# Loops written out, the last down and output projections by token chunk, five barriers out and x loaded at once, in a one-core decoder layer

## What is computed

```python
def layer(l, x, attend, x0_re, x0_im):
    x = x + 0.5 * swiglu(rmsnorm(x, g_ffn1[l]), w1_gate[l], w1_up[l], w1_down[l])
    h = rmsnorm(x, g_mix[l])
    q, k, v, qi, ki, wi, u, gates = jnp.split(h @ w_in[l], PROJ_SPLITS, axis=-1)
    o_a = attend(l, q, k, v, qi, ki, wi).reshape(b, t, D_ATTN)   # top-k sparse attention
    y_s, xr, xi = s5_scan(u, ...)                                 # state space branch
    y_s = jax.nn.gelu(y_s)
    o_b = y_s * jax.nn.sigmoid(y_s @ w_glu[l] + b_glu[l])
    g_a, g_b = jnp.split(jax.nn.sigmoid(gates), 2, axis=-1)
    merged = g_a * (o_a @ w_pa[l]) + g_b * (o_b @ w_pb[l])
    x = x + merged @ w_out[l]
    x = x + 0.5 * swiglu(rmsnorm(x, g_ffn2[l]), w2_gate[l], w2_up[l], w2_down[l])
    return x, (k, v, ki, xr, xi)
```

## Time and profile before

| | |
|---|---|
| Median of 3 runs | 3167.9 us (3166.7 to 3173.63) |
| Profiled execution, span from first to last instruction | 3174.7 us |
| PE busy | 2761.3 us, 87% of the span |
| DVE, ACT, POOL busy | 42%, 22%, 26% |
| Chain that ended last, by engine | PE 54%, DVE 11%, issue 3%, ACT 3% |
| Executed instructions | 40,963 |

### The profile page before, as it was taken

The page is one execution under the profiler, slowest core; times in us unless marked ns, Lnnn a source line. Parts: engine busy times, 40 slices in busy tenths (PEclk is TensorE's granted clock), DMA queues, the critical chain, the costliest instruction groups (busy, mean ns, idle before and its releaser), DMA issues.

```text
span 3174.7 us, 40963 instructions
## 1 busy us (share of the span) xinstructions
PE 2761.3 (87%) x16047; PEld 2514.3 (79%) x16047; DVE 1319.7 (42%) x2743; ACT 688.8 (22%) x1195; POOL 817.9 (26%) x521
## 2 busy tenths in 40 slices
PE   5999999999679999956689845688879999999996
PEld 4999999999658999944444544577869999999995
DVE  2223222222338999958731355133351222222224
ACT  4211111110133333313332410221041111111103
POOL 2522233232231112224300060022143232322210
PEclk8999999999889999976689555598989999999998
DMA  3211111110211322232222011142011111111101
GB/s 93 67 40 41 41 48 60 40 53 13 97 27 54 93 80 93 87 146 80 80 106 80 29 11 16 45 174 80 14 49 58 41 56 52 41 53 40 41 14 54
DMA packets 182798, 189.56 MB, mean 60 GB/s; under 512 B 18524, under 2 KB 164176, under 8 KB 179784
## 3 DMA queue, kind: packets, MB, share of 16 engines
q1 hardware_dynamic: 162632, 133.19, 14.0%
q0 software_dynamic: 2944, 35.65, 3.0%
q10 hardware_dynamic: 17072, 18.51, 1.6%
HBM read 160.10 MB, written 25.78 MB: 59 GB/s over the span
## 4 chain that ended last, share of the span: by engine, by line
PE 54%; DVE 11%; issue 3%; ACT 3%; DMA 1%; POOL 1%; SPq 0%; ACTq 0%; DVEq 0%; POOLq 0%
PE ps L232 15%; PE ps L574 12%; PE ps L248 8%; PE ps L1822 3%; PE ps L1808 3%; PE ps L1205 2%; PE ps L802 2%; DVE k_index_T_high L1122 1%; PE ps L824 1%; DVE new_small L1120 1%; PE ps L1522 1%; DVE probs L848 1%; PE ps L1562 1%; PE ps L1492 1%; PE ps L1520 1%
## 5 line engine op out<-in xcount | busy, mean ns | idle before, releaser
L232 PE MATMUL ps<-normed_split,f_weights_split 128*128 128x344 f32 x6336 | 1016.0, 323 | 26.0 <-issue 13.9
L232 PEld LDWEIGHTS ps<-normed_split,f_weights_split 128*128 128x128 f32 x6336 | 1011.0, 190 | 28.9 <-issue 15.3
L248 PE MATMUL ps<-f_hidden_split,f_down_split 128*128 128x344 f32 x3168 | 505.1, 321 | 11.9 <-issue 11.9
L248 PEld LDWEIGHTS ps<-f_hidden_split,f_down_split 128*128 128x128 f32 x3168 | 502.1, 189 | 12.4 <-issue 12.4
L279 DVE TENSOR_TENSOR f_hidden<-f_silu,ps 128x344 f32<-128x344 f32 x132 | 67.7, 513 | 877.3 <-PE ps L232 868.9
L574 PE MATMUL ps<-normed_split,in_weights_split 128*128 128x344 f32 (+1 forms) x2520 | 408.1, 323 | 14.8 <-POOL normed_split L110 13.6
L574 PEld LDWEIGHTS ps<-normed_split,in_weights_split 128*128 128x128 f32 (+1 forms) x2520 | 399.9, 188 | 19.3 <-POOL normed_split L110 14.3
L289 DVE SCALAR_TENSOR_TENSOR x_T<-ps,x_T 128x344 f32<-128x344 f32 x528 | 272.9, 517 | 232.5 <-PE ps L248 232.4
L196 POOL TENSOR_TENSOR f_hidden_split<-f_hidden,f_hidden_split 128x344 fp32r<-128x344 f32 x132 | 122.7, 930 | 595.4 <-DVE f_hidden_split L282 595.4
L188 POOL TENSOR_TENSOR f_weights_split<-f_weights_raw,f_weights_split 128x1024 fp32r<-128x1024 f32 x88 | 210.3, 2410 | 81.9 <-ACT f_weights_split L150 81.9
L202 POOL TENSOR_TENSOR f_down_split<-f_down_raw,f_down_split 128x1024 fp32r<-128x1024 f32 x44 | 104.2, 2388 | 436.2 <-ACT f_down_split L166 436.2
(11 more groups left out here) (303 smaller groups left out, 2624.7 us busy)
## 6 DMA issues: line engine op xcount, KB each, us to landing
f_weights_raw<-in_w_gate SPq DMA_DIRECT2D x44, 512.0 KB, 3.9
f_weights_raw<-in_w_up SPq DMA_DIRECT2D x44, 512.0 KB, 4.2
f_down_raw<-in_w_down SPq DMA_DIRECT2D x44, 512.0 KB, 3.5
in_weights_raw<-in_w_in SPq DMA_DIRECT2D x34, 512.0 KB, 3.8
gates_T<-projected ACTq DMA_DIRECT2D x16, 516.0 KB, 2.6
gates<-gates_T SPq DMA_DIRECT2D x16, 516.0 KB, 4.5
x_meanwhile<-x_T SPq DMA_DIRECT2D x1, 4128.0 KB, 15.1
x_T<-x_meanwhile SPq DMA_DIRECT2D x1, 4128.0 KB, 17.7
```

The source lines that it names most:

```text
L232: mm = nc.tensor.matmul(m.ps[:, NCH * half + c, :CH], m.wh[:, 2 * e + half, a, k * P:(k + 1) * P], m.xn[:, k, b, cols(c)], start=(k == 0 a ...
L248: mm = nc.tensor.matmul(m.ps[:, 6 + n % 2, :CH], m.dh[:, e, a, o * P:(o + 1) * P], m.hh[:, 2 * par + e, b, cols(c)], start=(e == 0 and t = ...
```

## The change

1. **Loops written out.** All `Fori` loops of the feed-forward blocks and of the input projection become straight code on all engines. The order of the work in them is the same.
2. **Last down projection by chunk.** `down(10)` of both blocks goes chunk by chunk (c outside, o inside) through five PSUM banks. From its second chunk on, each group of six matmuls is followed by one of the next norm's sums (`norm_sum`). Its weights are split into free room of the gate and up weights (`wh`), once `gate_up(20)` has ended. DVE adds the third chunk's groups between the multiplications of the next norm's first chunk. "d3" of the output projection likewise.
3. **Norm order on ACT.** Squares run 11 ahead, then one square follows each high part.
4. **Output stage.** The output weights have two buffers, and their splits stand earlier in the streams of SP, ACT and POOL (`SPLITS`); PE keeps `ORDER`.
5. **Barriers** 1, 2, 3, 7 and 8 go; semaphores on x (`ffn_x_ready`, `out_x_ready`) and on the last uses of memory take their place.
6. **Start.** x has a buffer for each block, so all loads are issued at once, the page table behind them on SP; the gains move to ACT's queue. The sums of chunk 0 stand between the turns of blocks 5 and 6. The 8 gathers of POOL move from barrier 3 to the start, ahead of the first weight splits.
7. **End.** The final norm starts in the last down projection; ACT does all its squares and roots ahead of the row copies, and there are four row buffers.

The diff, cut to its core:

```diff
+LAST = NPAIR - 1
+LAST_BANKS = (0, 1, 2, 6, 7)
+SUM_BANK = 3
...
+def norm_act(nc, act, m, s, ready, before=lambda n: None):
+
+    def square(n):
+        c, k = divmod(n, KD)
+        ready(act, c, k)
+        if n >= 3:
+            act.wait_ge(s.sum, s.was.sum + n - 2)
+        nc.scalar.activation(m.sg[:, n % 3, :], m.x[:, k, cols(c)], ACT.Square).then_inc(s.sq, 1)
+
+    for n in range(KD + 3):
+        square(n)
     for c in range(NCH):
         act.wait_ge(s.var, s.was.var + c + 1)
         nc.scalar.activation(m.rstd[:, 1, :], m.rstd[:, 0, :], ACT.Sqrt).then_inc(s.std, 1)
         for k in range(KD):
             n = c * KD + k
             act.wait_ge(s.xn, s.was.xn + n + 1)
             nc.scalar.activation(m.xn[:, k, 0, cols(c)], m.hf[:, n % 3, :], ACT.Copy).then_inc(s.hi, 1)
-
+            if n + KD + 3 < NCH * KD:
+                square(n + KD + 3)
...
+def norm_sum(nc, pe, m, s, n, bank=SUM_BANK):
+    c, k = divmod(n, KD)
+    pe.wait_ge(s.sq, s.was.sq + n + 1)
+    nc.tensor.matmul(m.ps[:, bank + c, :CH], m.ones[:], m.sg[:, n % 3, :],
+                     start=(k == 0), stop=(k == KD - 1)).then_inc(s.sum, 1)
...
+def norm_dve(nc, dve, m, s, gain, bank=SUM_BANK, between=lambda k: None):
     for c in range(NCH):
+        norm_rstd(nc, dve, m, s, c, bank)
         for k in range(KD):
+            if c == 0:
+                between(k)
...
-    def down(p, par, used=True):
+    def down_one(p, o, c, bank, w):
+        for e in range(2):
+            for t, (a, b) in enumerate(PASSES):
+                mm = nc.tensor.matmul(m.ps[:, bank, :CH], w[:, e, a, o * P:(o + 1) * P],
+                                      m.hh[:, (2 * p + e) % 4, b, cols(c)],
+                                      start=(e == 0 and t == 0), stop=(e == 1 and t == 2))
+        mm.then_inc(s.down, 1)
+
+    def down(p):
...
-    with pe.Fori(0, (NPAIR - 3) // 2) as i:
-        for q in range(2):
-            f = 4 * i + 2 * q + 6
-            gate_up(f, 0)
-            gate_up(f + 1, 1)
-            down(2 * i + q + 2, q)
-    down(NPAIR - 1, 0)
+                down_one(p, o, c, 6 + n % 2, m.dh)
+
+    def down_last():
+        pe.wait_ge(s.hlo, s.was.hlo + NCH * NF)
+        pe.wait_ge(s.dlo, s.was.dlo + NF)
+        for n in range(NCH * KD):
+            c, o = divmod(n, KD)
+            if n >= 3:
+                pe.wait_ge(s.acc, s.was.acc + NCH * KD * LAST + n - 4)
+            down_one(LAST, o, c, LAST_BANKS[n % 5], m.wh)
+            if c:
+                next_sum(n - KD)
+        for k in range(KD):
+            next_sum((NCH - 1) * KD + k)
+
+    for f in range(NF):
+        gate_up(f)
+        if f % 2 and f > 1:
+            down(f // 2 - 1)
+    down_last()
 
...
+    for f in range(NF):
+        hidden(f)
+        if f % 2 and f > 1:
+            accumulate(f // 2 - 1)
+    for n in range(2 * KD):
+        ffn_accumulate_last(nc, dve, m, s, n)
...
+SPLITS = (0, 1, 2, "d0", 3, 4, "d1", 5, 6, "d2", 7, "d3")
...
+    odd = sb("out_weights_split_odd", [P, 2, 2, D], F32R)
-    m.dh = sb("out_weights_split", [P, 2, 2, D], F32R)
+    m.dh = (sb("out_weights_split", [P, 2, 2, D], F32R), odd)
...
-                if p:
-                    act.wait_ge(s.down, NCH * KD * p)
-                nc.scalar.activation(m.dh[:, e, 0, :], m.dr[:, e, :], ACT.Copy).then_inc(s.dhi, 1)
+                if p >= 2:
+                    act.wait_ge(s.down, NCH * KD * (p - 1))
+                nc.scalar.activation(m.dh[p % 2][:, e, 0, :], m.dr[:, e, :], ACT.Copy).then_inc(s.dhi, 1)
...
             for n in range(NCH * KD):
-                o, c = divmod(n, NCH)
-                if p or n >= 2:
+                o, c = divmod(n, NCH) if p < 3 else (n % KD, n // KD)
+                if p < 3 and (p or n >= 2):
                     pe.wait_ge(s.acc, NCH * KD * p + n - 1)
+                if p == 3 and n >= 3:
+                    pe.wait_ge(s.acc, NCH * KD * p + n - 4)
+                bank = 6 + n % 2 if p < 3 else LAST_BANKS[n % 5]
+                if p == 3 and c:
+                    next_sum(n - KD)
+    for k in range(KD):
+        next_sum((NCH - 1) * KD + k)
...
+            if p == 3:
+                for n in range(2 * KD):
+                    out_accumulate_last(nc, dve, m, s, n)
+                continue
...
 def in_sp(nc, sp, m, s, i):
-    for n, g in enumerate(i.gains):
-        sp.dma_start(m.grow[KD * n:KD * (n + 1), :], g.rearrange("(k p) -> k p", p=P)).then_inc(s.gain_in, 16)
     for b in range(NB + 1):
         rows = P if b < NB else TS
-        if b >= 2:
-            sp.wait_ge(s.turned, 2 * (b - 1))
         src = i.x_prompt[b * P:(b + 1) * P, :] if b < NB else i.x_sample
-        sp.dma_start(m.xin[:rows, b % 2, :], src).then_inc((s.x_in0, s.x_in1)[b % 2], 16)
+    rows = PAGE // PER_ROW
+    for j in range(N_PAGES):
+        sp.dma_start(m.pages[rows * j:rows * (j + 1), :],
...
+def in_pe(nc, pe, m, s, first_sum):
+    for b in range(6):
+        in_turn(nc, pe, m, s, b)
+    for k in range(KD):
+        first_sum(k)
+    for b in range(6, NB + 1):
+        in_turn(nc, pe, m, s, b)
+    for n in range(KD, NCH * KD):
+        first_sum(n)
+    pe.wait_ge(s.kept, 2 * NB + 2)
...
+def in_act(nc, act, m, s, i):
+    for n, g in enumerate(i.gains):
+        act.dma_start(m.grow[KD * n:KD * (n + 1), :], g.rearrange("(k p) -> k p", p=P)).then_inc(s.gain_in, 16)
...
+    for n in range(KD + 3):
+        square(n)
+    root(0)
+    for n in range(KD + 3, 2 * KD + 3):
+        square(n)
+    root(1)
+    for n in range(2 * KD + 3, NCH * KD):
+        square(n)
+    root(2)
...
+        if b >= 4:
+            act.wait_ge(s_io.y_out[b % 4], s_io.y_from[b % 4] + 16 * (b // 4))
...
+            in_act(nc, act, m_in, s_io, i)
+
+            def blocks_of_x(n):
+                if n in (0, 3, KD):
+                    for b in range(3):
+                        in_keep(nc, act, m_in, s_io, 3 * (0, 3, KD).index(n) + b)
+                if n == KD:
+                    for half in range(2):
+                        ffn_act_split(nc, act, m_f1, s_f1, 0, half)
+            norm_act(nc, act, m_f1, s_f1, x_in_ready, blocks_of_x)
...
+            pool.wait_ge(s_io.steps, 3)
+            for b in range(TS):
+                smp_load(pool, m_mix, b, m_mix.kidx[:, b], i.cache_kidx, s_io.ki_in)
+            for half in range(2):
+                ffn_pool_split(nc, pool, m_f1, s_f1, 0, half)
+            norm_pool(nc, pool, m_f1, s_f1)
             ffn_pool(nc, pool, m_f1, s_f1)
...
+            pool.wait_ge(s_f1.down, NCH * KD * NPAIR)
             nc.gpsimd.memset(m_mix.bias01[:], 0.0).then_inc(s_io.leave, 1)
...
+            in_pe(nc, pe, m_in, s_io, lambda n: norm_sum(nc, pe, m_f1, s_f1, n, 4))
+            ffn_pe(nc, pe, m_f1, s_f1, lambda n: norm_sum(nc, pe, m_mix, s_nm, n))
+            proj_pe(nc, pe, m_mix, s_mix, s_nm)
             barrier(pe, 1)
```

728 lines of the change are left out of this document (321 added, 407 removed).

## The result

The changed kernel takes 3034.7 us (median of 4 runs, 3033.7 to 3036.8), the kernel before in the same comparison 3168.1; the ratio is 0.9564 (95% interval 0.9542 to 0.9585). That is 133 us won where 151 were forecast: the time lies in the range of the prediction, 18 us above the forecast of 3016.9. The profiled execution has a span of 3032.1 us and a time of 3033.9, so 1.8 us of a time lie outside the span; PE is busy for 2741.1 us (90%), and 38,694 instructions were executed.

The account below looks back on a forecast made before the run. PE was taken as the bound, time to be had only at its stops: jumps, output-projection parts and four norms. Six terms, 23.3 + 36.2 + 34.3 + 18.6 + 19.8 + 18.8 = 151.0, took 3167.9 to 3016.9 us; range 2998 to 3046.

Parts of the forecast that it names:

- A: Feed-forward loops: straight code removes PE's stops at jumps back and the slow matmuls after them; 23.3 us, bounds 18 and 25.
- the first part: Opening on what bounds the kernel: stage differences against the profiled execution, span 3174.7 us, are carried over to the median.
- B: Output stage: earlier weight splits with two buffers remove PE's waits ahead of "d0" to "d3" and slow starts; 36.2 us.
- C: Norm between FFN1's last down projection and the input projection: sums between matmuls, no split wait; 34.3 us, bounds 29 and 38.
- D: Norm from "d3" of the output projection to FFN2's first gate tile: shorter chain; 18.6 us, bounds 14 and 22.
- E: Program's end, from FFN2's last down projection through the final norm and stores: shorter; 19.8 us, bounds 14 and 23.
- T0: Last projection before a norm: moment when chunks 0 and 1 with 8 sums end, put at its start S + 19.9.
- F: Program's start up to gate tile 0's end: x loaded at once, first norm earlier; 18.8 us, bounds 8 and 22.
- rival (1): Start: POOL's gathers hold the first norm up, POOL reaching it at 52 instead of 41.5; 3027 us, chance 0.13.
- Rival (2): Interleaved groups and sums: PE's clock falls, about 11 us more in each of C, D and E; 3050 us, chance 0.10.
- (4): Loops: the jumps weren't the cause, stops recur at the same places and A is nothing; 3040 us, chance 0.05.
- rival (3): Written-out code: not fetched in time, each added packet stops PE like a jump; about 3490 us, chance 0.03.

Follow-up runs that it names:

- PE's loop alone: The changed kernel with the hardware loop put back on PE alone in both feed-forward blocks, other engines keeping straight code; 3051.4 us.
- the second one: The kernel before, unchanged, profiled once more; 3166.0 us, span of the profiled execution 3165.9.
- one buffer: The changed kernel with one buffer for the split output weights, split at the old place in the streams of SP, ACT and POOL; 3070.0 us.
- the sums behind: The changed kernel with all 24 next-norm sums behind the last group of the last down and output projections, all additions to x ahead of the norm; 3052.0 us.
- the gathers later: The changed kernel with POOL's 8 gathers moved from the start into FFN1, one behind each of hidden tiles 1 to 8; 3026.7 us.
- the run with 12 spare matmuls: The changed kernel with 12 spare matmuls ahead of the last index projection, gaps ahead of the scores left empty; 3024.4 us, the profiled execution 3006.9.

## Why the prediction was right, and where it was off

**A, right in mechanism, of uncertain size.** The stops are PE's jumps (24.8 us with PE's loop alone), and straight code has none. The size is no constant: 23.3 in the execution read, 16.7 in the second one (10.1 of stops and 4 slow starts), 24.8 with PE's loop alone. The step that failed is the last one of the first part, "I carry the difference over to the median": the terms were read in an execution 8.4 us above the median, and a large part of that was the term itself.

**B, right.** 34.6 in the trace, 35.3 by undoing it, 36.2 forecast. The difference is mostly that "d0" and "d1" hold PE for 23.4 us each (0.50 of it the wait for DVE) and "d2" for 23.0, where 22.8 was taken.

**C, D and E, right step by step.** Ahead of the input projection T0, POOL's three starts, the twelfth sum and the last sum all came within 0.3 us of the forecast. In E the last products end at T0 + 27.3 (27.7) and the program at T0 + 35.2 (35.4). D is 2.4 over its term, since gate tile 0 ran at 22.8 us, at the full clock, where 9.4 was taken for its first chunk, the time at the lower one, and the last sum came at T0 + 24.0. The interleaving is worth 17 us of the three, measured; how order by chunk, the free split and the missing barriers share the other 59 was not tested.

**F, right in its size by luck.** The forecast had POOL and the norm's chain ready together, at 41 and 41.5. POOL was (41.25), by two errors that met: its gathers began at 23.6 and not at 26, and the eighth stopped for 3.24, for which nothing was put. The chain was not: the first high part was done at 33.9, 7 us sooner, since DVE's inversion ended at 32.7 and not at 40.5. So the gathers did hold the first norm up, which is rival (1), not by the stop of the eighth (3.24 us, not 10.6) but by standing there at all; the price is 8.0 us by the run that moved them. What the loads at once and the other edits of the start are worth by themselves was not tested.

**Rival (2) had the right thing at the wrong place.** The clock did not fall among the interleaved groups, as the stretch from the start of the last projection to the end of its groups shows, here in C (D and E have 1.00 there too):

```profile
784.00:817.00 33.00, 31.80 (x177) 28.54 (x176) 19.39 (x34) 12.42 (x25) 6.23 (x6) 1.00 0.00 1
```

It fell 60 us later, in the scores, and cost 10.9. The prediction looked for a lower clock only where the change moves instructions; the scores were not touched, and so no term and no rival spoke of them.

**Rivals (3) and (4) fell.** Straight code shows no idle time without a releaser; the queue that answers to the earlier trace rows has 126 packets, for 119 before, where rival (3) had estimated some 96 more:

```profile
q8 instruction: 126, 2.06, 0.3%
```

In sum, of the 17.6 us between forecast (151.0) and measurement (133.4), 11.4 are losses outside the terms (10.9 of them the scores' clock) and 9.2 the two executions read; the terms gave 3.1 back (0.1 is rounding).

## What to carry to other kernels

Write an engine's long loop out where that engine is the bound, and put the reductions of the next stage between the last matmuls of this one; cost such a chain instruction by instruction from the profile: ahead of the input projection it came out within a microsecond. Check each input of it as well, since the start's chain was 7 us off by the same way of reckoning. Don't carry a difference of spans over to a median before a second execution has been seen: where stops at jumps come and go, one profile can be 8 us off. And list each stretch of narrow or broken PE work behind the change, even an untouched one: its clock may come out at the other level.

## What the runs showed of the hardware

PE's clock in unchanged work is a matter of its own. The 40 score matmuls ran at 1.00 in eight of the traces named above (27 to 28 us from the first to the last) and at 0.50 for most of the stretch in four (38 to 40 us: the changed kernel and the runs with one buffer, with the sums behind and with the gathers later), with the same score instructions. In three of the eight spare matmuls fill the gaps; in the other five the gaps are those of the four. Nor did the level ahead decide: the dense projection in front began at the lower clock in the kernel before (24.52 us) and in the run with the gathers later (24.48, where the changed kernel has 22.96), and the scores behind it ran at 1.00 in the first and at 0.50 in the second. Once down, the clock stayed at 0.50 although PE was busy: here in the tail of attention, behind the 32 one-column matmuls, first in the changed kernel and then in the run with 12 spare matmuls, where it rose again and the stage became 17 us shorter (716.3 instead of 733.6):

```profile
1700.00:1720.00 20.00, 20.00 (x59) 11.30 (x59) 5.83 (x26) 9.81 (x25) 0.00 (x0) 0.50 0.00 0
1720.00:1740.00 20.00, 20.00 (x62) 11.37 (x61) 6.08 (x30) 11.10 (x32) 0.00 (x0) 0.50 0.01 1
```

```profile
1690.00:1710.00 20.00, 19.01 (x91) 11.18 (x90) 9.16 (x42) 14.86 (x38) 0.00 (x0) 0.89 0.00 1
1710.00:1730.00 20.00, 17.40 (x86) 9.57 (x84) 9.82 (x55) 17.10 (x56) 0.00 (x0) 1.00 0.00 0
```

A PE that is busy for all 20 us of a slice is here the slow one: at 0.50 it has 59 and 62 matmul records in a slice, at 0.89 and 1.00 it has 91 and 86 and waits a little. What decides between the two levels the runs leave open.
